# The first gate/up tile of each feed-forward as plain products, with one weight sum moved from an adding DMA to VectorE

## The chip, the cores and the metric

The kernel runs on one core of a Trainium2 chip. The metric is the device time of one execution in microseconds, as the median of several runs. The engines are named as in the profile: PE is TensorE (PEld its weight loads), DVE is VectorE, ACT is ScalarE, POOL is GpSimd, SP is SyncE, which here only issues DMAs.

## What is computed

A trunk of two layers over 512 tokens of width 1024, all in float32. Each layer is: half a feed-forward, a mixer, half a feed-forward.

```python
for layer in range(DEPTH):                      # DEPTH = 2
    x = x + FFN_RES * swiglu_ffn(rms_norm(x, ffn1_norm[layer]), ffn1_w_gate_up[layer], ffn1_w_down[layer])
    h = rms_norm(x, mix_norm[layer])
    y = swa_sink_attention(...) if kind == 0 else mla_attention(...)
    x = x + y
    x = x + FFN_RES * swiglu_ffn(rms_norm(x, ffn2_norm[layer]), ffn2_w_gate_up[layer], ffn2_w_down[layer])
return rms_norm(x, final_norm)

def swiglu_ffn(x, w_gate_up, w_down):           # 1024 -> 2 x 2816 -> 1024
    g, u = jnp.split(x @ w_gate_up, 2, axis=-1)
    return (jax.nn.silu(g) * u) @ w_down
```

So there are four feed-forwards, numbered f = 0 to 3 in the code, and two mixers between them.

## The kernel before

**Precision.** Every matmul operand is split in two parts: a high part that ACT writes by a copy (`high_fill`, `high_direct`, `high_mixed`) and a low part, the operand minus the high one, that DVE writes (`low_fill`, `low_direct`, `low_mixed`). A product is three matmuls: high by high, high by low, low by high (L1803 to L1805).

**Seven products in place of eight.** A feed-forward is cut into 30 units (`ffn_units`): 22 "G" units, each a tile of 128 gate and 128 up columns, and 8 "D" units of the down matrix, in the order G0-9, D, D, D, D, G10-17, D, D, D, D, G18-21. Within a unit the four weight blocks and the four quarters of the activations are combined by sums so that seven products (q = 1 to 7) of 128x256 columns replace eight: 7 x 4 chunks x 3 = 84 matmuls. The weight sums are made in SBUF. Four raw blocks per unit come from HBM: three lie in `plain` (loaded by SP in two DMAs, 512 and 256 KB), the fourth is loaded into `chain` and once more into `single`. POOL issues DMAs that add a further block to these (`accum_op`): three in turn to `chain` (`link`, steps 0, 1, 2; L754), one to `single` (`join`; L762). Each of the six weight operands of a unit is one fill: FA (two blocks, 128x1024) and FC from `plain`; FU, FB and FD from `chain` after its first, second and third sum; FE from `single`.

**Activations.** `h_mix` holds for each of four pairs of 128-column chunks three direct quarters and four sums of quarters (`mix`, three instructions on DVE, `x_sums`), each as high and low part. `pair_split` makes them in the order sums 0 and 1, direct low part, sum 2; then `high_mixed` (ACT) and `low_mixed` (DVE) split the sums.

**Order of the work.** It is written out by hand, and every engine runs its own list in order. On TensorE a unit is the products 1(u), 2(u), 4(u-1), 6(u), 3(u-1), 5(u), 7(u). In unit u DVE makes the low parts FU(u+1), FA(u+1), FC(u), FB(u+1), FD(u), FE(u+1), with the gate and up arithmetic in between; ACT writes the high parts in the same order, the copies s_1, u_2, u_3 of products 1, 6 and 7 (L957, L970, L991) that let the next product be added into the same bank, and the silu. Product 6 waits for s_1, product 7 for u_2, product 4 of the next unit for u_3. In eight units per feed-forward (3, 5, 7, 9, 14, 17, 19, 21, `COMBINED`) the hidden tiles of two G units are turned into direct quarters and sums for the D units, which adds `mix`, `high_direct`/`low_direct` and `high_mixed`/`low_mixed`.

**The beginning of a feed-forward.** `pairs_out` (ACT and DVE) evacuates the eight blocks that end the stage before: DVE adds a block to `xT` (L1297), ACT scales it with the gain (`gained`, L886) into `x_pair`, which has two buffers, and squares it for the norm; after each second block the pair is split. FA(0) and FU(0) are filled at the last block, ahead of its evacuation. TensorE runs the products 1, 2, 5 of unit 0 in `ffn`, then `sums` (the sum of squares, L1854), products 6 and 7, then `spread` (L1864), which brings the reciprocal root of the norm (POOL's `power`, then four small DVE instructions, `rms_values`) to all partitions, and goes on with unit 1. The first feed-forward has no stage before it: the tokens are loaded by DMA, transposed on TensorE (`x_transposed`, L1901) between the products of unit 0, and split in the same way.

**The down blocks and the rest of the weights** (`load`, `high`, `low`) pass through raw slots `w_raw`, which lie in `r_all`, the memory that also holds `plain`, `single` and the rotary tables; so their loads wait for the last fills of a feed-forward, and the first `plain` loads of the next one wait for the last splits of blocks. SP issues all these loads in order.

Of the kernel before, what the change touches and what calls it, by code (L numbers as in the profile page):

```python
# [13 lines left out]
P = 128  # L14
# [59 lines left out]
def fill_count(f, kind, u):  # L74

    at = {FU: 6 * u - 2 if u else 1, FA: 6 * u - 1 if u else 0, FB: 6 * u + 1 if u else 2, FE: 6 * u + 3,
          FC: 6 * u + 6 - 2 * (u == NU - 1), FD: 6 * u + 8 - 3 * (u == NU - 1)}[kind]
    return 6 * NU * f + at + 1


def product_order():
    out = [(q, 0) for q in (1, 2, 5, 6, 7)]
# [8 lines left out]
def product_count(f, q, u):  # L91

    return 7 * NU * f + PRODUCTS[q, u] + 1


def half_order():
    out = []
    for u in range(1, NU + 1):
        if u == 1:
            out.append((0, 0))  # L100
        if u < NU and UNITS[u][0] == "G":
            out.append((u, 0))
        if UNITS[u - 1][0] == "G":
            out.append((u - 1, 1))
# [6 lines left out]
def silu_order():  # L111
    out = []
    for u in range(1, NU):
        if u > 1 and UNITS[u - 2][0] == "G":
            out.append((u - 2, 1))
# [8 lines left out]
def half_count(f, u, half):  # L124

    return 2 * TILES * f + HALVES[u, half] + 1
# [5 lines left out]

def chain_count(f, u, steps):

    return 16 * (3 * ((NU * f + u) // CHAIN) + steps)


def single_count(f, u, steps):

    return 16 * ((NU * f + u) // SINGLE + steps)  # L140
# [144 lines left out]
def kv_interleaved(w, slot):  # L285

    return kv_raw(w, slot).rearrange("p (r t f) -> p r t f", t=2, f=HD)
# [21 lines left out]
def build(nc, x, gains, weights, a_sinks, consts, out):  # L309
# [3 lines left out]
    with ExitStack() as ctx:  # L313
# [52 lines left out]
        y_hi, y_lo = rows_of(y_all, 0, KD, S), rows_of(y_all, BIG, KD, S)  # L366
        h_mix, y_mix = (v[:, :].rearrange("p (k q l n) -> p k q l n", k=7, q=PAIRED, l=2) for v in (h_all, y_all))
# [4 lines left out]
        tables = r_flat[:, 8 * S:11 * S]  # L372
# [10 lines left out]
        x_pair = [view(4 * S + i * 2 * S, 4, HN) for i in range(2)]  # L383
        x_sum = view(8 * S, 4, HN)
        g_0 = [view(10 * S + i * HN, HN) for i in range(2)]
        g_1 = view(11 * S, HN)
        c_22 = [view(11 * S + (1 + i) * HN, HN) for i in range(2)]
        s_1, u_3 = view(11 * S + 3 * HN, HN), view(13 * S, HN)
# [45 lines left out]
        single_in = [sem(f"single_in{i}") for i in range(SINGLE)]  # L434
        chain_sum = [sem(f"chain_sum{i}") for i in range(CHAIN)]
        single_sum = [sem(f"single_sum{i}") for i in range(SINGLE)]
# [32 lines left out]
        gr_done = sem("gr_done")  # L469
        silu_done = sem("silu_done")  # L470
# [107 lines left out]
        def _(sp):  # L578
# [8 lines left out]
            def load_chain(f, u):  # L587

                g = NU * f + u
                if g >= CHAIN:  # L590
                    sp.wait_ge(fill_lo, fill_count((g - CHAIN) // NU, FD, (g - CHAIN) % NU))
# [6 lines left out]
            def load_single(f, u):  # L598

                g = NU * f + u  # L600
                if g >= SINGLE:
                    sp.wait_ge(fill_lo, fill_count((g - SINGLE) // NU, FE, (g - SINGLE) % NU))
                sp.dma_start(single[u % SINGLE], unit_source(f, u, A_21)).then_inc(single_in[u % SINGLE], 16)

            def load_plain(f, u):
# [3 lines left out]
                elif f > 0:  # L609
                    for i in ((3,), (0, 1), (1, 2))[u]:  # L610
                        sp.wait_ge(split_done, max(n for n in range(SEG_AT[f - 1], SEG_AT[f]) if slot(n) == i) + 1)
# [4 lines left out]
            def load_unit(f, u):  # L616

                if u == 0:
                    if f > 0:
                        sp.wait_ge(fill_lo, fill_count(f - 1, FC, NU - 3))  # L620
                    if f == 1:
                        sp.wait_ge(rot_done, 1 + PAIRS)
                        sp.wait_ge(t1_done, 1 + PAIRS)
                    if f == 3:
                        sp.wait_ge(mq_ready, 2)
                if f == 0 and u == 0:
                    load_plain(f, u)
                    load_x(2)
                    load_chain(f, u)
# [1559 lines left out]
```

## Time and profile before

| | us |
|---|---|
| three runs, median (lowest to highest) | 1867.21 (1865.55 to 1869.53) |
| profiled execution, its own time | 1863.95 |
| span of the profiled execution, first to last instruction | 1862.2 |
| PE busy | 1736.1 |
| DVE busy | 1424.5 |
| ACT busy | 962.8 |
| POOL busy | 447.9 |

The span lies in the profiled execution; the rest of its time is around it. PE busy counts a pipelined matmul from start to modelled end. The four feed-forwards take from the start to 362 us, 533 to 859, 904 to 1231 and 1486 to 1817 (without their down blocks); the mixers and the down blocks lie between them.

### The profile page before, as it was taken

What the parts mean: (1) busy time and instruction counts of PE and PEld (TensorE: products, weight loads), DVE (VectorE), ACT (ScalarE), POOL (GpSimd) and SP (SyncE); (2) the same over time, 40 slices, a digit from 0 to 9 for tenths busy, and PEclk for the clock granted to TensorE, in tenths of its full rate; (3) what the DMA queues carried; (4) which work ended last, traced back from release to release, by engine and by line L of the source; (5) the groups of instructions that cost most, each with busy time, mean ns of one, the idle gap of its engine ahead of it and who ended that gap; (6) DMA issues with size and microseconds to landing.
All of it is one profiled execution on the core that took longest, in us unless ns stands there. A gap on an engine that the chain in (4) does not pass through costs nothing. (4 is left out here: it accounts for less than half of the span.)

```text
span 1862.2 us, 34651 instructions
## 1 busy us (share of the span) xinstructions
PE 1736.1 (93%) x12889; PEld 1621.8 (87%) x12889; DVE 1424.5 (76%) x2796; ACT 962.8 (52%) x1904; POOL 447.9 (24%) x511
## 2 busy tenths in 40 slices
PE   5999999999969999999699999999999789999997
PEld 4999999977869999998599999987867689999995
DVE  5788787768668878866688778666896578878788
ACT  4554554446555545544455455444565455545452
POOL 1333333111023333330233333300000033333320
PEclk6999999999989999999899999999999899999999
DMA  6899999543359999993699999945112489999961
GB/s 177 204 214 235 230 221 231 151 113 86 108 128 231 221 227 229 223 204 107 163 231 218 223 221 229 212 117 130 29 42 66 117 190 219 224 224 224 231 157 69
DMA packets 189956, 329.42 MB, mean 177 GB/s; under 512 B 24865, under 2 KB 58846, under 8 KB 189790
## 3 DMA queue, kind: packets, MB, share of 16 engines
q0 software_dynamic: 69120, 125.86, 39.6%
q1 hardware_dynamic: 119104, 199.60, 33.9%
q8 instruction: 105, 1.72, 0.4%
q10 hardware_dynamic: 1566, 1.74, 0.3%
q14 instruction: 61, 0.50, 0.1%
HBM read 320.58 MB, written 2.10 MB: 173 GB/s over the span
## 5 line engine op out<-in xcount | busy, mean ns | idle before, releaser
L1803 PE MATMUL bank<-h_all,w_all 128*128 128x256 f32 x2464 | 711.6, 289 | 76.6 <-issue 28.7
L1804 PE MATMUL bank<-h_all,w_all 128*128 128x256 f32 x2464 | 704.9, 286 | 0.0
L1805 PE MATMUL bank<-h_all,w_all 128*128 128x256 f32 x2464 | 704.5, 286 | 0.0
L1803 PEld LDWEIGHTS bank<-h_all,w_all 128*128 128x128 f32 x2464 | 480.8, 195 | 88.3 <-issue 63.5
L1804 PEld LDWEIGHTS bank<-h_all,w_all 128*128 128x128 f32 x2464 | 481.0, 195 | 0.0
L1805 PEld LDWEIGHTS bank<-h_all,w_all 128*128 128x128 f32 x2464 | 480.8, 195 | 0.0
L754 POOL DMA_DIRECT2D work<-ffn_gu x264 | 231.7, 925 | 831.7 <-DVE w_all L1187 549.2
L868 ACT ACTIVATE w_all<-work 128x512 fp32r<-128x512 f32 x360 | 213.2, 622 | 322.1 <-DMA work<-ffn_gu 200.4
L1187 DVE TENSOR_TENSOR w_all<-work,w_all 128x512 fp32r<-128x512 f32 x360 | 243.9, 686 | 120.3 <-ACT w_all L868 120.1
L1187 DVE TENSOR_TENSOR w_all<-r_all,w_all 128x512 fp32r<-128x512 f32 (+1 forms) x360 | 310.7, 863 | 25.4 <-ACT w_all L868 20.1
L868 ACT ACTIVATE w_all<-r_all 128x512 fp32r<-128x512 f32 (+1 forms) x360 | 275.2, 767 | 84.9 <-PE bank L1805 84.1
L1803 PE MATMUL bank<-y_all,w_all 128*128 128x256 f32 x896 | 254.4, 284 | 11.4 <-DVE w_all L1187 11.4
L1804 PE MATMUL bank<-y_all,w_all 128*128 128x256 f32 x896 | 253.5, 283 | 0.0
L1805 PE MATMUL bank<-y_all,w_all 128*128 128x256 f32 x896 | 253.5, 283 | 0.0
L1803 PEld LDWEIGHTS bank<-y_all,w_all 128*128 128x128 f32 x896 | 171.9, 192 | 12.9 <-DVE w_all L1187 12.8
L1804 PEld LDWEIGHTS bank<-y_all,w_all 128*128 128x128 f32 x896 | 171.9, 192 | 0.0
L1805 PEld LDWEIGHTS bank<-y_all,w_all 128*128 128x128 f32 x896 | 171.9, 192 | 0.0
L945 ACT ACTIVATE work<-work 128x256 f32<-128x256 f32 x176 | 73.0, 417 | 143.7 <-DVE work L1354 143.4
L754 POOL DMA_DIRECT2D work<-ffn_d x96 | 87.3, 984 | 167.1 <-DVE w_all L1187 166.8
L1174 DVE TENSOR_TENSOR w_all<-r_all,w_all 128x1024 fp32r<-128x1024 f32 (+2 forms) x76 | 73.9, 972 | 57.2 <-ACT w_all L846 51.7
L762 POOL DMA_DIRECT2D r_all<-ffn_gu x88 | 86.3, 980 | 121.6 <-issue 120.8
L1341 DVE SCALAR_TENSOR_TENSOR xT<-bank,xT 128x256 f32<-128x256 f32 x224 | 93.7, 418 | 21.6 <-PE bank L1805 20.4
(186 smaller groups left out, 2591.3 us busy)
## 6 DMA issues: line engine op xcount, KB each, us to landing
work<-ffn_gu POOLq DMA_DIRECT2D x264, 256.0 KB, 5.8
r_all<-ffn_gu SPq DMA_DIRECT2D x88, 512.0 KB, 5.2
r_all<-ffn_gu SPq DMA_DIRECT2D x176, 256.0 KB, 5.9
work<-ffn_d POOLq DMA_DIRECT2D x96, 256.0 KB, 6.0
work<-ffn_gu SPq DMA_DIRECT2D x88, 256.0 KB, 5.6
r_all<-ffn_gu POOLq DMA_DIRECT2D x88, 256.0 KB, 6.9
r_all<-ffn_d SPq DMA_DIRECT2D x64, 256.0 KB, 5.6
r_all<-ffn_d SPq DMA_DIRECT2D x32, 512.0 KB, 5.2
```

The costliest lines, as they stand in the source:

```text
L754: pool.dma_start(chain[g % CHAIN], unit_source(f, u, slice(part * S, (part + 1) * S)), accum_op=ALU.add).then_inc(chain_sum[g % CHAIN], 16)
L762: pool.dma_start(single[u % SINGLE], unit_source(f, u, slice(0, S)), accum_op=ALU.add).then_inc(single_sum[u % SINGLE], 16)
L868: a.activation(hi, src, ACT.Copy).then_inc(fill_hi, 1)
L945: a.activation(buf, buf, ACT.Silu).then_inc(silu_done, 1)
L1174: last = v.tensor_tensor(w_lo[:, sl, 0:k, 0:m], w_raw[:, sl, 0:k, 0:m], w_hi[:, sl, 0:k, 0:m].bitcast(F32), ALU.subtract)
L1187: v.tensor_tensor(lo, src, hi.bitcast(F32), ALU.subtract).then_inc(fill_lo, 1)
L1341: return v.scalar_tensor_tensor(at, src, -0.5 if c < PAIRED else 0.5, at, ALU.mult, ALU.add)
L1803: t.matmul(o, wh, xh, start=c == 0 and not on, stop=False, skip_group_check=on)
L1804: t.matmul(o, wh, xl, start=False, stop=False, skip_group_check=on)
L1805: last = t.matmul(o, wl, xh, start=False, stop=c == PAIRED - 1, skip_group_check=on)
```

## The change

Unit 0 of each feed-forward (the first gate/up tile) is no longer made by the seven products. TensorE gets a new function that makes the gate tile and then the up tile, each 128x512, as plain products: 4 chunks x 2 blocks x 2 halves x 3 = 48 matmuls each. It needs only FA, FU and FC of unit 0, all of them raw blocks, and no sums of quarters; of the activations it needs the three direct quarters and the fourth quarter, which is split on its own into a new place, `early`, in `y_all`.

```diff
+            def plain_tile(f, up):
+                b = (C_BANKS if up else B_BANKS)[0]
+                pe.wait_ge(fill_lo, fill_count(f, FU if up else FA, 0))
+                if up:
+                    pe.wait_ge(fill_lo, fill_count(f, FC, 0))
+                places = ((1, 1), (2, 0)) if up else ((0, 0), (0, 1))
+                for c in range(PAIRED):
+                    if not up:
+                        pe.wait_ge(direct_lo, combine_count(f, c, False))
+                        pe.wait_ge(early_lo, PAIRED * f + c + 1)
...
             def ffn(f, m, ready):
-                if f > 0:
-                    pe.wait_ge(evac_done, ready - 2)
-                    for q in (1, 2, 5):
-                        product(f, q, 0, (0, PAIRED - 1))
-                    for q in (1, 2, 5):
-                        product(f, q, 0, (PAIRED - 1, PAIRED))
+                plain_tile(f, False)
                 sums(m, KD)
-                product(f, 6, 0)
-                product(f, 7, 0)
-                spread(m + 1)
+                plain_tile(f, True)
                 if f > 0:
                     pe.wait_ge(evac_done, ready)
-                for u in range(1, NU):
+                product(f, 1, 1)
+                spread(m + 1)
+                for q in (2, 6, 5, 7):
+                    product(f, q, 1)
+                for u in range(2, NU):
```

In `pairs_out` FA(0) moves one block ahead, FC(0) and the join of unit 1 are added, the sums of a pair (`pair_mix`) come after the direct and early parts of `pair_split`, and a mixed split comes after the evacuation of a block, not ahead of it. What is left of the last pair's sums and the fills of unit 1 move into `begin`, behind the end of `pairs_out`.

```diff
                 for j in range(KD):
                     if j >= begun:
                         low(n + j + AHEAD, end)
+                    if j == KD - 2:
+                        low_fill(f, FA, 0)
                     if j == KD - 1:
-                        low_fill(f, FA, 0)
                         low_fill(f, FU, 0)
-                    if j >= 3 and j % 2:
-                        q = (j - 3) // 2
-                        low_mixed(h_mix, combine_count(f, q, False), q)
+                        join(f, 1)
                     b = product(n + j)
                     v.scalar_tensor_tensor(xT[:, PERM[j], :], b[:, :], factor, xT[:, PERM[j], :],
                                            ALU.mult, ALU.add).then_inc(evac_done, 1)
+                    if j >= 3 and j % 2 and j < KD - 1:
+                        q = (j - 3) // 2
+                        low_mixed(h_mix, combine_count(f, q, False), q)
+                    if j >= 2 and j % 2 == 0:
+                        pair_split(f, j // 2 - 1)
+                        pair_mix(f, j // 2 - 1)
                     if j:
                         added(j == 1)
...
+            def begin(f, m):
+                def first():
+                    low_mixed(h_mix, combine_count(f, PAIRED - 1, False), PAIRED - 1)
+                    low_fill(f, FA, 1)
+                low_fill(f, FU, 1)
+                join(f, 2)
+                rms_values(m, D, first)
+                low_fill(f, FB, 1)
+                low_fill(f, FE, 1)
```

The gate of unit 0 is then normed over its whole width (`first_gate`), goes through silu on ACT and is multiplied with the up tile (`first_hidden`), all in unit 1. The first feed-forward has four pair buffers in place of two; its transposes run ahead of the tile, and its sums of pairs come behind all direct parts.

In the other units the sum of FE, an adding DMA of POOL onto a second load of the fourth block, becomes one DVE instruction: `chain` plus a block of `plain` into `single`. The second load goes too. As the first link changes `chain`, POOL's first link of a unit waits for this `join`; before, it waited only for the load of `chain`.

```diff
-            def load_single(f, u):
...
-                sp.dma_start(single[u % SINGLE], unit_source(f, u, A_21)).then_inc(single_in[u % SINGLE], 16)
...
                 if step == 0:
-                    pool.wait_ge(chain_in[g % CHAIN], 16 * (g // CHAIN + 1))
+                    pool.wait_ge(joined, order_of(f, u) + 1)
...
+            def join(f, u):
+                g = NU * f + u
+                dve.wait_ge(chain_in[g % CHAIN], 16 * (g // CHAIN + 1))
+                dve.wait_ge(plain_in[(u + 2) % 3], unit_count(f, u))
...
+                v.tensor_tensor(single[u % SINGLE], chain[g % CHAIN], plain[(u + 2) % 3][:, 0:S], ALU.add
+                                ).then_inc(joined, 1)
...
                     low_fill(f, FA, u + 1)
+                    join(f, u + 2)
```

The raw slots of the blocks move from `r_all` to `x_f`, except for the last segment. Their loads wait for the last product 7 of the D units, and the first `plain` loads of the next feed-forward wait for fills of this one instead of splits of blocks. The rotary tables (768 KB after the first feed-forward, 256 KB after the third) are loaded one unit later and ahead of the blocks.

```diff
-        w_raw = r_all[:, 0:SLOTS, :].rearrange("p s (k m) -> p s k m", m=P)
+        w_raw = x_f[:, :, :].rearrange("p a s -> p (a s)").rearrange("p (s k m) -> p s k m", s=SLOTS, m=P)
...
-                    sp.wait_ge(fill_lo, fill_count(f, FE, NU - 2))
+                    sp.wait_ge(fill_lo, fill_count(f, FE, NU - 1))
                     sp.dma_start(tables[:, part * S:3 * S], consts[:, P + part * S:]).then_inc(t_in, 16)
```

The remaining lines of the diff renumber counters and semaphores to the new order.

## Rows read from the trace of the kernel before

**Rows 1.** The page: span, and busy time with share and instructions of each engine
```profile
span 1862.2 us, 34651 instructions
...
PE 1736.1 (93%) x12889; PEld 1621.8 (87%) x12889; DVE 1424.5 (76%) x2796; ACT 962.8 (52%) x1904; POOL 447.9 (24%) x511
```

**Rows 2.** Waits of TensorE: line, releaser, us in total, times, longest
```profile
PE bank L1803 <- issue: 28.7, 5, 10.5
...
PE bank L1803 <- ACT work L991: 25.1, 27, 1.8
...
PE bank L1864 <- DVE st L1261: 12.5, 3, 4.6
```

**Rows 3.** Windows: busy us of PE, PEld, DVE, ACT, POOL; PEclk, DMA share
```profile
560.00:620.00 60.00, 59.99 (x501) 59.81 (x500) 50.39 (x98) 35.31 (x69) 20.87 (x24) 1.00 0.98 229
...
893.60:934.20 40.60, 23.68 (x157) 23.13 (x157) 27.62 (x48) 19.33 (x33) 10.78 (x12) 0.79 0.77 181
```

**Rows 4.** Timeline of TensorE: start, us, operation [idle before <- releaser]
```profile
47.04 1.84 PE L1854 MATMUL bank<-ones,acc 128*128 128x1 f32 x8 [5.66 <-DVE acc L1230]
...
65.86 0.28 PE L1803 MATMUL bank<-h_all,w_all 128*128 128x256 f32 x1
...
524.79 0.39 PE L1760 MATMUL bank<-y_all,w_all 128*128 128x512 f32 x1
...
562.74 0.28 PE L1803 MATMUL bank<-h_all,w_all 128*128 128x256 f32 x1
...
893.22 0.39 PE L1760 MATMUL bank<-y_all,w_all 128*128 128x512 f32 x1
...
904.08 0.55 PE L1803 MATMUL bank<-h_all,w_all 128*128 128x256 f32 x1 [10.47 <-issue]
...
921.57 1.12 PE L1864 MATMUL bank<-ident,st 128*128 128x128 f32 x4 [4.58 <-DVE st L1261]
...
934.21 0.28 PE L1803 MATMUL bank<-h_all,w_all 128*128 128x256 f32 x1
...
1476.68 0.39 PE L1760 MATMUL bank<-y_all,w_all 128*128 128x512 f32 x1
...
1515.54 0.28 PE L1803 MATMUL bank<-h_all,w_all 128*128 128x256 f32 x1
```

**Rows 5.** Timeline of ACT and DVE at the third beginning
```profile
900.72 1.06 ACT L875 ACTIVATE h_all<-work 128x1024 fp32r<-128x1024 f32 x1 [1.89 <-DVE work L1203]
...
902.75 1.22 DVE L1187 TENSOR_TENSOR w_all<-r_all,w_all 128x1024 fp32r<-128x1024 f32 x1 [2.07 <-ACT w_all L868]
...
905.63 0.68 DVE L1297 SCALAR_TENSOR_TENSOR xT<-bank,xT 128x512 f32<-128x512 f32 x1
```

**Rows 6.** DMA queues and issues of 960:1000, then 533:541
```profile
q0 software_dynamic: 2168, 3.94, 57.9%
...
q1 hardware_dynamic: 2106, 4.89, 37.8%
...
work<-ffn_gu POOLq DMA_DIRECT2D x12, 256.0 KB, 5.8
...
work<-ffn_gu POOLq DMA_DIRECT2D x1, 256.0 KB, 3.7
```

**Rows 7.** Timeline of DVE and ACT over two units
```profile
979.86 0.68 DVE L1187 TENSOR_TENSOR w_all<-work,w_all 128x512 fp32r<-128x512 f32 x1
...
980.47 0.42 DVE L1398 TENSOR_TENSOR work<-bank,work 128x256 f32<-128x256 f32 x1
...
985.45 1.16 ACT L868 ACTIVATE w_all<-work 128x512 fp32r<-128x512 f32 x2 [2.19 <-DMA work<-ffn_gu]
...
986.11 0.69 DVE L1187 TENSOR_TENSOR w_all<-work,w_all 128x512 fp32r<-128x512 f32 x1 [1.17 <-ACT w_all L868]
...
989.02 0.69 DVE L1187 TENSOR_TENSOR w_all<-work,w_all 128x512 fp32r<-128x512 f32 x1
...
1000.95 0.68 DVE L1187 TENSOR_TENSOR w_all<-work,w_all 128x512 fp32r<-128x512 f32 x1
```

More of the change, by code:

```diff
@@ L91, in product_count @@
 def product_count(f, q, u):
[L93 removed]
+    return len(PRODUCTS) * f + PRODUCTS[q, u] + 1
 def half_order():
@@ L112, in silu_order @@
     out = []
-    for u in range(1, NU):
-        if u > 1 and UNITS[u - 2][0] == "G":
+    for u in range(2, NU):
+        if u > 2 and UNITS[u - 2][0] == "G":
             out.append((u - 2, 1))
@@ L948, in ffn @@
                 end = SEG_AT[f + 1]
-                for u in range(NU):
-                    gate, before = UNITS[u][0] == "G", u > 0 and UNITS[u - 1][0] == "G"
-                    at = NU * f + u
+                begin(f)
+                for u in range(1, NU):
+                    gate, before = UNITS[u][0] == "G", u > 1 and UNITS[u - 1][0] == "G"
+                    at = order_of(f, u)
                     b = B_BANKS[u % 2]
@@ L961, in ffn @@
                     if u == 1:
-                        silu(f, 0, 0)
-                    if gate and u > 0:
+                        act.wait_ge(z_gate, f + 1)
+                        a.activation(z_0, z_0, ACT.Silu).then_inc(z_silu, 1)
+                    if gate:
                         silu(f, u, 0)
@@ L1790, in product @@
                     b = B_BANKS[u % 2]
-                fresh = u == 0 or (not gate and UNITS[u - 1][0] == "G")
+                fresh = u == 1 or (not gate and UNITS[u - 1][0] == "G")
                 for c in range(*part):
@@ L1807, in product @@
                     last.then_inc(prod_done, 1)
[L1809 to L1815 removed]
+            def plain_tile(f, up):
[8 more added lines that the diff above has]
+                        pe.wait_ge(early_lo, PAIRED * f + c + 1)
+                    for e, (i, j) in enumerate(places):
+                        wh, wl = (w_all[:, i, low, j * S + c * P:j * S + (c + 1) * P] for low in range(2))
+                        for half in range(2):
+                            o = b[:, half * HN:(half + 1) * HN]
+                            if half and not e:
+                                xh, xl = early[:, c, 0, :], early[:, c, 1, :]
+                            else:
+                                d = D_B11 if not e else (D_B22 if half else D_B21)
+                                xh, xl = h_mix[:, d, c, 0, :], h_mix[:, d, c, 1, :]
+                            first, end = c == 0 and not e and not half, c == PAIRED - 1 and e == 1
+                            t.matmul(o, wh, xh, start=first, stop=False, skip_group_check=half == 1)
+                            t.matmul(o, wh, xl, start=False, stop=False, skip_group_check=half == 1)
+                            last = t.matmul(o, wl, xh, start=False, stop=end, skip_group_check=half == 1)
+                        if c == PAIRED - 1 and (e or up):
+                            last.then_inc(prod_done, 1)
```

290 lines of the change are left out of this document (163 added, 127 removed).

## Prediction

> **What bounds the kernel now.** I read the page first: TensorE is busy for 1736 of 1862 us, so any gain has to come from its gaps or its work [rows 1]. The TensorE waits tell where the gaps are [rows 2]: 28.7 us in five waits of up to 10.5 us and 12.5 us in three waits for `st`, nearly all where a feed-forward begins, and 25.1 us in 27 small waits for ACT's copy u_3 (L991), spread over the units. Between those, a stretch of 60 us holds 501 matmuls [rows 3]: one takes 0.12 us, a unit of 84 takes 10.08 us, and nothing can be won there. In the same stretch the DMA engines are at 0.98: saturated, though TensorE does not wait for them directly.
>
> The third feed-forward shows a beginning [rows 4]: the last matmul of the block before starts at 893.22 (it ends at 893.6), unit 0 begins at 904.08 after 10.47 us idle, the spread of the norm waits another 4.58 us, and unit 2 begins at 934.21. That is 40.6 us for 144 matmuls worth 17.3. A matmul lasts 0.55 us at 904.08 and 0.28 us at 934.21: the granted clock over this stretch is 0.79 [rows 3], so part of it runs at the lower level, 1.2 GHz, after the idle time. From last matmul to unit 2 the second feed-forward takes 37.6 us (525.2 to 562.74), the fourth 38.5 (1477.1 to 1515.54); the first reaches unit 2 at 65.86 [rows 4].
>
> Why TensorE stands there is in DVE's and ACT's rows [rows 5]. The first weights (FA) get their low part at 902.75, because ACT split the third pair's sums first (900.72, 1.06 us, itself 1.89 us behind DVE's last sum). DVE evacuates the last block only at 905.63, twelve us after TensorE finished it.
>
> **The change, part by part.** *TensorE's work.* Unit 0 goes from 84 to 96 matmuls: 12 x 0.12 = 1.44 us in each feed-forward, 5.8 in all, all on the path; it is inside the sums below.
>
> *The beginnings.* The plain tile needs no sums of a pair, only the pair and one early quarter of it. I walk through the third one with durations of the rows (start to start: 0.60 us for 128x512 on DVE, 0.34 for 128x256, 0.87 for the direct part, 1.13 for 128x1024; ACT 0.5 to 1.0), in the new program order. FA is split one block sooner, at 897.8, so TensorE starts near 897.9, after some 4.8 us idle, and goes through pairs 0 to 2. The last evacuation comes at 904.0 (before: 905.63; FA, FU, the new join at 0.60 and two early splits are ahead of it, one mixed split is not). Then gain 0.7, ACT direct and early 1.2, DVE direct and early 1.3 with their handovers: pair 3 is ready at 907.5. TensorE's last quarter (12 matmuls at the lower level after the wait, an estimated 0.12 x 0.55 / 0.28 = 0.23 each: 2.8), the sums (0.9) and the up tile (1.4 for six slow matmuls, 5.0 for the rest) end near 917.6. The norm is computed under the up tile: DVE's values at 912.6, POOL's power by 914.5, four small steps by 915.7. So the 4.58 us wait for the spread should vanish. Products 1, spread and 2 of unit 1 end near 921.0, 6 and 5 near 924; product 7 waits about 1 us for ACT, which has the new full-width gate in front (norm, silu). Unit 2 begins near 926.3: 7.9 us earlier than 934.21. The second and fourth have the same chain behind their last evacuation, and a table load for silu in it (1.3 us); the same steps give 556.7 and 1509.7 against 562.74 and 1515.54: 6.0 and 5.8. In the first, the transposes no longer stand behind products and the sums of squares end at 42.5; before, TensorE's sums began at 47.04 after waiting 5.66 for them [rows 4]; unit 2 comes at about 61.0 instead of 65.86: 4.8. Sum: 24.5 us. Bounds: were there no waits at all, the third would need 20.2 us instead of 40.6, the other three about as much, and the gain would be near 75; were the pair order to cost DVE more than it frees, it could fall to some 8.
>
> *DMA removed.* Per unit one plain load of 256 KB and one adding DMA go. In a saturated window of 40 us the adding queue moved 3.94 MB (15 DMAs) in 57.9% of the engines' time, 1.54 us each; the plain queue 4.89 MB (18.7 pieces of 256 KB) in 37.8%, 0.81 each [rows 6]. Per unit 4 x 1.54 + 5 x 0.81 = 10.2 us of 10.08 becomes 3 x 1.54 + 4 x 0.81 = 7.9: from saturated to 78%. An adding DMA lands 5.8 us after its issue in the loaded window, 3.7 with nothing else in flight [rows 6]. I take 4.0 for the change, near the idle end, since the moved link finds little else in flight.
>
> *The join on DVE.* A 128x512 instruction with two SBUF operands lasts 0.69 us and 0.61 from start to start (979.86, 980.47) [rows 7]; 29 units x 4 = 116 of them, 70 us of DVE. DVE is the tight engine where units with pair sums (3, 5, 7, 9 and 14, 17, 19, 21) alternate with plain ones: from FU's low part to the next FU it takes 9.16 us (979.86 to 989.02) and then 11.93 (to 1000.95), 21.09 a pair against TensorE's 20.16 [rows 7]; the excess is what L991's waits show, 6 pairs x 4 with about 1 us. In the plain unit DVE idles 1.17 us before 986.11, because ACT waited for the adding DMA of FB until 985.45 [rows 7]. The join takes 0.60 in each unit: in the plain one it fits into that idle time if the DMA lands sooner, in the other it adds in full (12.53).
>
> *The moved link.* The first adding DMA of unit u+2 used to be issued behind the one before it on POOL's queue; now it waits for the join, 3.2 us after FU's low part, and ACT's FU of the next unit waits for its landing. Queued behind ACT's wait are s_1 (TensorE's product 6 waits for it) and FA; behind POOL's, the third link, which is not due. The loop is 3.2 + 0.35 wake-up + landing + 0.75 on ACT + 0.6 on DVE: 4.9 + landing. At 4.0 it is 8.9, a pair is 8.9 + 12.5 = 21.4, 1.25 over TensorE; x 24 pairs = 30 us, 5 more than now. Against that, the irregular waits for late DMAs behind the 25.1 (units outside this pattern, most of them in the fourth feed-forward) should go: about 8. Steady units: -3, say 0, with 24 us for each us of landing: 3.7 gives -10, 4.7 +14, 5.8 +40.
>
> The Trainium skill says (DMA: Bandwidth & Descriptors, "Latency and other measured facts") that a DMA's fixed cost shrinks when HBM is lightly loaded; the two landings of [rows 6] agree in direction. Its fit for a DMA issued from GpSimd ("Anatomy of one DMA") would give an estimated 2.6 us for 256 KB, under the 3.7 of the row; with it the loop would be 7.5 us and never bind.
>
> *Raw blocks in other memory.* The down blocks' loads start earlier; nothing waits for them now. The rotary tables after the first and third are loaded a unit later and ahead of the first block: in the first (768 KB) ACT waits for that block in unit 29, and u_2 and product 7 behind it; 1 to 3 us, I take 2, in the third none. Early splits on ACT and DVE (0.34 each, 16 of them) are in the walk above. The SP queue loses a load and the waits before it: free.
>
> Sum against the profiled execution, 1863.95 us by its time (span 1862.2): 1863.95 - 24.5 + 0 + 2 = 1841.5. The median of the runs is 3.3 above the profiled one, so 1845 for a median.
>
> **Rivals.** *The link behind the join binds (slower).* Place: ACT's FU of every plain unit. It decides from the landing at which steady units lose the 22 us that the beginnings win: (25 + 8 + 22) / 24 = 2.3 us a pair, a loop near 9.95, a landing of 5.0 without the 8 us, 4.7 if late DMAs stay. At the loaded 5.8 the pair is 23.2: 73 us of waits instead of 25, 1890. For it: the landing is 5.8 today, the plain loads start 1.5 us after the join. Against: a fifth of the DMA time is gone. Chance 0.14.
>
> *The relief wins in the steady units too.* Landing falls to 3.7: the loop is 8.6, DVE alone binds (8.4 + 12.53 = 20.93), 0.8 to 0.95 a pair, and the irregular waits go: -10, to 1835, with better beginnings (a DVE that is less far behind) 1825. Chance 0.22.
>
> *The wait is only moved at the beginnings.* The DVE and ACT chain that evacuates the blocks stays; if pair 3 comes at the old 909, or the clock stays low through the up tile (42 matmuls more at 0.23 instead of 0.12: 4.6 us), each beginning gains 2 to 3: 10 us in all, 1860 to 1865. Chance 0.14.
>
> **How the numbers follow.** The forecast, 1845, has 0.50; its own range is 1836 to 1856. Range for 8 in 10: 1827 to 1872, from the good end of the relief to the link at a landing of 4.9. A difference of about 0.2% (3.7 us) is what a measurement of this kernel can tell from none. Faster: 0.50 + 0.22 + half of the moved wait, less a little for the forecast's own tail, 0.76; same 0.10; slower 0.14.
>
> **What the profile after would show.** TensorE's wait before the first tile at 5 us or less, no wait for `st`, unit 2 some 8 us sooner in the third; DMA share near 0.8 in the steady stretches, adding DMAs landing at about 4; waits for L991 of about 1 to 1.5 us after units 5, 7, 9, 17, 19, 21. Waits of TensorE for s_1 (L957 before) and of ACT for `work` at FU would mean that the link binds; first waits still of 8 us and a low clock through the up tile, that the beginnings did not move.

## The result and the profile after

The change made the kernel slightly slower: 1873.36 us against 1868.64 us, medians of 20 runs each, taken beside one another, ratio 1.0027 with a 95% interval of 1.0016 to 1.0038. I had forecast 1845, faster. By the bound that I gave (0.2%) this is slower, and it lies above my range.

The page of the changed kernel: span, busy times, the two DMA queues (packets, MB, share of 16 engines' span) and two landings:

```profile
span 1872.5 us, 34649 instructions
...
PE 1750.5 (93%) x12937; PEld 1634.8 (87%) x12937; DVE 1484.5 (79%) x2892; ACT 958.6 (51%) x1892; POOL 331.1 (18%) x379
...
q0 software_dynamic: 50112, 91.25, 29.1%
q1 hardware_dynamic: 101824, 168.13, 28.9%
...
work<-ffn_gu POOLq DMA_DIRECT2D x252, 256.0 KB, 4.6
...
work<-ffn_d POOLq DMA_DIRECT2D x96, 256.0 KB, 5.0
```

TensorE's longest waits in it (line, releaser, us in total, times, longest), to be read beside [rows 2]:

```profile
PE bank L1881 <- ACT work L1011: 33.0, 29, 2.0
PE bank L1881 <- DVE w_all L1207: 16.5, 12, 1.4
PE bank L1908 <- DVE y_all L1252: 14.7, 5, 5.4
PE bank L1956 <- DVE acc L1274: 14.7, 1, 14.7
PE bank L1908 <- DVE w_all L1207: 10.2, 3, 4.8
```

The waits for `st` and the waits of 10.5 us are gone, as intended; the 14.7 us at L1956 lie in the first feed-forward, where TensorE comes to the sums of squares sooner and waits for them longer (5.66 us before, [rows 4]). The wait for u_3 (L1011, before L991) rose from 25.1 to 33.0 us.

Where the time went can be read from the starts of the matmuls: a unit is 84 of them, so every 84th start of L1881 to L1883 is the start of a unit. I use five sums over the four feed-forwards: "beginnings" is the time from the last block's end (in the first: from zero) to unit 2; the others are what units take over 10.08 us each. "D units" stands for 10 to 13 and 22 to 28: eight D units and the G units that follow the second group; "29" is unit 29. In us, from one profiled execution of every kernel of this study:

| kernel | ratio to before [95%] | beginnings | units 2–9 | 14–21 | D units | 29 |
|---|---|---|---|---|---|---|
| before | 1 | 182.5 | 12.8 | 9.0 | 23.6 | 4.5 |
| the change | 1.0027 [1.0016, 1.0038] | 166.6 | 24.6 | 7.4 | 34.4 | 8.5 |
| plain_tile_alone | 0.9916 [0.9894, 0.9937] | 161.0 | 16.8 | 12.6 | 23.7 | 9.5 |
| join_alone | 1.0014 [0.9994, 1.0034] | 173.8 | 15.8 | 8.3 | 37.5 | 4.5 |
| join_own_copy | 0.9933 [0.9910, 0.9956] | 165.5 | 19.9 | 6.6 | 27.5 | 8.3 |
| join_on_pool | 1.0150 [1.0124, 1.0176] | 162.1 | 33.8 | 19.3 | 38.9 | 9.8 |
| plain_tile_tables | 0.9886 [0.9856, 0.9916] | 159.7 | 15.5 | 13.2 | 25.1 | 4.5 |
| hybrid_tables | 0.9827 [0.9803, 0.9851] | 161.5 | 14.9 | 4.0 | 23.8 | 4.5 |
| join_sooner | 0.9933 [0.9912, 0.9954] | 163.2 | 17.3 | 6.6 | 31.5 | 9.7 |
| spare_add | 0.9960 [0.9944, 0.9976] | 155.7 | 23.6 | 12.4 | 28.0 | 9.7 |
| after_filled | 0.9983 [0.9968, 0.9998] | 159.6 | 26.8 | 11.9 | 31.6 | 7.0 |
| hybrid_filled | 0.9811 [0.9793, 0.9830] | 152.7 | 16.8 | 3.3 | 26.1 | 4.5 |

Between the two profiled executions the span grew by 10.3 us: beginnings −15.9, units +25.2, the rest +1.0. By the medians the difference is 4.7 us; the profiled execution of before lies 4.7 us under its median of these runs, that of the changed kernel 1.0 above its own, so about half of the 10.3 is scatter between executions. Single cells scatter too: after_filled, which differs from the change at the beginnings alone, has 2.2 us more in units 2–9, 4.4 more in 14–21 and 2.9 less in the D units. I rest on ratios, and on cells only where several kernels say the same.

### The profile page after: what moved, and what is told of

It is laid out like the page before. It is cut to its first block and busy times, and to the rows that moved or that the text cites. A ratio compares the mean times of both kernels' runs of the same rounds, so it can differ in the third digit from the quotient of the medians.

```text
span 1872.5 us, 34649 instructions
## 1 busy us (share of the span) xinstructions
PE 1750.5 (93%) x12937; PEld 1634.8 (87%) x12937; DVE 1484.5 (79%) x2892; ACT 958.6 (51%) x1892; POOL 331.1 (18%) x379
## 5 line engine op out<-in xcount | busy, mean ns | idle before, releaser
L1881 PE MATMUL bank<-h_all,w_all 128*128 128x256 f32 x2352 | 670.7, 285 | 42.3 <-ACT work L1011 33.0
L1882 PE MATMUL bank<-h_all,w_all 128*128 128x256 f32 x2352 | 666.7, 283 | 0.0
L1883 PE MATMUL bank<-h_all,w_all 128*128 128x256 f32 x2352 | 666.6, 283 | 0.0
L1881 PEld LDWEIGHTS bank<-h_all,w_all 128*128 128x128 f32 x2352 | 452.4, 192 | 50.0 <-issue 34.1
L1882 PEld LDWEIGHTS bank<-h_all,w_all 128*128 128x128 f32 x2352 | 452.8, 193 | 0.0
L1883 PEld LDWEIGHTS bank<-h_all,w_all 128*128 128x128 f32 x2352 | 452.6, 192 | 0.0
L766 POOL DMA_DIRECT2D work<-ffn_gu x252 | 219.8, 872 | 1014.6 <-DVE w_all L1207 513.9
L870 ACT ACTIVATE w_all<-work 128x512 fp32r<-128x512 f32 x352 | 209.3, 624 | 334.9 <-DMA work<-ffn_gu 203.3
L1207 DVE TENSOR_TENSOR w_all<-work,w_all 128x512 fp32r<-128x512 f32 x352 | 238.8, 687 | 100.9 <-ACT w_all L870 100.0
L1881 PE MATMUL bank<-y_all,w_all 128*128 128x256 f32 x896 | 256.2, 286 | 18.5 <-DVE w_all L1207 11.4
L1883 PE MATMUL bank<-y_all,w_all 128*128 128x256 f32 x896 | 253.3, 283 | 0.0
L1881 PEld LDWEIGHTS bank<-y_all,w_all 128*128 128x128 f32 x896 | 171.6, 191 | 24.4 <-DVE w_all L1207 16.9
L1883 PEld LDWEIGHTS bank<-y_all,w_all 128*128 128x128 f32 x896 | 171.7, 192 | 0.0
L1194 DVE TENSOR_TENSOR w_all<-x_f,w_all 128x1024 fp32r<-128x1024 f32 (+2 forms) x72 | 69.1, 959 | 61.0 <-ACT w_all L845 55.5
L1834 PE MATMUL bank<-y_all,w_all 128*128 128x512 f32 x272 | 107.3, 395 | 1.3 <-DVE w_all L1194 1.3
L1836 PE MATMUL bank<-y_all,w_all 128*128 128x512 f32 x272 | 106.0, 390 | 0.0
```

What stands on the lines that cost most here:

```text
L766: pool.dma_start(chain[g % CHAIN], unit_source(f, u, slice(part * S, (part + 1) * S)), accum_op=ALU.add).then_inc(chain_sum[g % CHAIN], 16)
L870: a.activation(hi, src, ACT.Copy).then_inc(fill_hi, 1)
L1194: last = v.tensor_tensor(w_lo[:, sl, 0:k, 0:m], w_raw[:, sl, 0:k, 0:m], w_hi[:, sl, 0:k, 0:m].bitcast(F32), ALU.subtract)
L1207: v.tensor_tensor(lo, src, hi.bitcast(F32), ALU.subtract).then_inc(fill_lo, 1)
L1834: t.matmul(b[:, :], wh, hi[:, c, :], start=c == 0, stop=False)
L1836: last = t.matmul(b[:, :], wl, hi[:, c, :], start=False, stop=c == k - 1)
```

## The experiments

Theories: (A) the join's time on DVE makes the units longer; (B) the units pay for the beginnings, because DVE and ACT enter unit 2 with work left over; (C) the first link, moved behind the join, comes too late.

### The plain tile without the join

```diff
-                    pool.wait_ge(joined, order_of(f, u) + 1)
+                    pool.wait_ge(chain_in[g % CHAIN], 16 * (g // CHAIN + 1))
...
+                pool.dma_start(single[u % SINGLE], unit_source(f, u, slice(0, S)), accum_op=ALU.add
+                               ).then_inc(single_sum[u % SINGLE], 16)
...
-                    join(f, u + 2)
```

> The changed kernel with FE's sum back where it was: a second load of the fourth block and an adding DMA of POOL; the first link waits only for its load again, DVE has no join. Between the two profiles the stretches from a feed-forward's start to its unit 2 got 15.9 us shorter in all, and the units from 2 to 29 got 25.3 us longer. Theory A (the join on DVE makes the units longer): the beginnings keep their 16 us, units 2 to 29 come back to the 1191 us of the kernel before, ratio 0.991 to 0.993. Theory B (the units pay for the beginnings: DVE and ACT enter unit 2 with work left over, whatever makes the join): units 2 to 9 stay some 10 us longer, ratio 0.997 to 1.000. The DMA share of a steady stretch goes back to 0.95 or more under both.

Measured: 0.9916, 1853.8 us. The beginnings are 21.5 us shorter than before. The D units are back at 23.7; units 2–9 keep 4.0 of their 11.8 us, and unit 29 is still 5.0 over before. So the plain tile, with the raw blocks in their new place, is good for some 16 us, and the other half of the change loses more than that. Mostly A or C, with a little of B.

### The join without the plain tile

```diff
+                dve.wait_ge(plain_in[(u + 2) % 3], unit_count(f, u))
...
+                v.tensor_tensor(single[u % SINGLE], chain[g % CHAIN], plain[(u + 2) % 3][:, 0:S], ALU.add
+                                ).then_inc(joined, 1)
...
+                    if u >= 2:
+                        pool.wait_ge(joined, joined_count(f, u))
```

> The kernel before with only the join of units 2 to 29 on DVE and the link behind it; beginnings, raw blocks and tables as they were. Theory A (join, or the link behind it): units 2 to 29 get 15 to 25 us longer, ratio 1.008 to 1.013. Theory B (the units pay for the beginnings): units 2 to 9 keep their 13 us of excess, only the D units and the last ones lose, 5 to 10 us, ratio 1.003 to 1.005. If the relief of the DMA engines is worth what my second rival said, ratio 0.995 or less.

Measured: 1.0014, and the interval takes in 1: less than A's or B's number, more than the relief's, so a miss for all three. The D units lose 14 us (the change: 10.9); units 2–9 lose 3.0, where the change loses 11.8. The beginnings gain 8.7 us in this profile, though nothing of them was moved: the wait for `st` is 7.9 us instead of 12.5; the reason is open. So in units 2–9 the parts don't simply add: the join costs little after the old beginnings and much after the new ones.

### The same join, with the link let go

```diff
-                    pool.wait_ge(joined, order_of(f, u) + 1)
+                    pool.wait_ge(chain_in[g % CHAIN], 16 * (g // CHAIN + 1))
...
-                v.tensor_tensor(single[u % SINGLE], chain[g % CHAIN], plain[(u + 2) % 3][:, 0:S], ALU.add
+                v.tensor_tensor(single[u % SINGLE], single[u % SINGLE], plain[(u + 2) % 3][:, 0:S], ALU.add
```

> The changed kernel, with the fourth block loaded a second time into the place of the sum, so that the join adds in place and the first link waits for its load alone, as in the kernel before. It takes one plain load of 256 KB per unit more (DMA share 0.77 to some 0.85). If the link behind the join costs (theory C), the units lose little or none of their 25 us, ratio 0.990 to 0.994; if the join's time on DVE costs (theory A) or the beginnings' leftover work (B), the ratio stays at 1.002 to 1.004.

Measured: 0.9933. With the join on DVE as in the change, and one load more, the kernel is 0.94% faster than the change: some 17.6 us. The released link is the one difference that lets work start sooner, so the price is the link's. C.

The loop itself can be read in a D unit of the changed kernel (third feed-forward). Timeline of DVE, ACT and POOL (start, us, operation, idle before and its releaser):

```profile
1037.26 0.68 DVE L1207 TENSOR_TENSOR w_all<-work,w_all 128x512 fp32r<-128x512 f32 x1
...
1040.76 0.69 DVE L1225 TENSOR_TENSOR r_all<-work,r_all 128x512 f32<-128x512 f32 x1
...
1048.18 0.69 DVE L1207 TENSOR_TENSOR w_all<-work,w_all 128x512 fp32r<-128x512 f32 x1 [0.76 <-ACT w_all L870]
...
1047.51 0.63 ACT L870 ACTIVATE w_all<-work 128x512 fp32r<-128x512 f32 x1 [1.16 <-DMA work<-ffn_d]
...
1041.85 0.86 POOL L766 DMA_DIRECT2D work<-ffn_d  x1 [2.68 <-DVE r_all L1225]
```

FU's low part at 1037.26, the join at 1040.76, the link at 1041.85; it lands 5.6 us later, when ACT, which has waited for it, starts FU of the next unit at 1047.51; DVE, which waits for ACT, follows at 1048.18. That is 10.9 us from FU to FU, where TensorE has 10.08. Over all 32 D units it is 10.36 us on average, but this average (and the landing of 5.45 us in it) mixes two kinds. In the first D unit of each group (10 and 22) the link lands in 3.7 us and nothing waits for it: 9.3 us. In the other 24 it is 10.71 us: 2.9 to the join, 0.7 of join, 0.4 to the link, a landing of 6.03 (5.64 to 6.55), and 0.7 for ACT and the handover; ACT idles 1.76 us and DVE 1.35 us ahead of FU. In the plain units of the pairs (6, 8, 18, 20) the landing is 3.9 on average and DVE idles 0.3 us. Over units 3 to 29, ACT's idle time ahead of FU is 64 us in the change, 11 before and 0 in join_own_copy; DVE's, ahead of FU's low part, is 48 us in the change, 6 before; ahead of FB's it fell from 109 to 37: the stall changed its place.

### The join sooner

```diff
                     low_fill(f, FU, u + 1)
+                    if u > 2 and u not in COMBINED:
+                        join(f, u + 2)
...
-                    join(f, u + 2)
+                    if u <= 2 or u in COMBINED:
+                        join(f, u + 2)
```

> The changed kernel with the join directly behind FU's low part in the units without pair sums, instead of behind FA's, some 2.4 us sooner; FA and the join wait for the first plain load alone, FC for the second. In the changed kernel the D units last 10.33 and 10.39 us from FU to FU, with 1.0 us of DVE idle ahead of FU: the loop over the moved link is 3.0 (FU to join) + 0.6 + 0.4 + 5.45 (landing) + 0.8. If that loop is the cost (theory C), it falls to about 8 us, the idle time goes and the kernel comes to 1857 to 1862, ratio 0.993 to 0.996, near join_own_copy. If DVE's time for the join is the cost (theory A), 1.001 to 1.004 as it is.

Measured: 0.9933, as C says. The same D unit, DVE and ACT:

```profile
1035.43 0.68 DVE L1208 TENSOR_TENSOR w_all<-work,w_all 128x512 fp32r<-128x512 f32 x1
1036.03 0.69 DVE L1226 TENSOR_TENSOR r_all<-work,r_all 128x512 f32<-128x512 f32 x1
...
1045.52 0.68 DVE L1208 TENSOR_TENSOR w_all<-work,w_all 128x512 fp32r<-128x512 f32 x1
...
1044.45 0.61 ACT L871 ACTIVATE w_all<-work 128x512 fp32r<-128x512 f32 x1
```

No engine waits at FU any more; the period is 10.09 us. (So that the join can come so early, FA and the join wait here for the first of the two plain loads alone, in every unit; this is not separated from the earlier join.) DVE's idle time ahead of FU in units 3 to 29 falls from 48 to 3 us. Units 2–9 gain 7.3 us, the D units 3.0 (with the link free altogether 4.7 and 7.0). Unit by unit the loop's share is plainer: units 11 to 13 and 23 to 25, the D units behind the first of each group, are over 10.08 us by 5.4 us in all in the change, 7.7 in join_alone and 4.5 in after_filled, by 0.2 or less before, in join_own_copy, in join_sooner and in spare_add, and by at most 1.4 in any other kernel. Two different ways of making the link earlier gave the same 0.9933: C holds, and its place is the loop over FU.

### The price of the join's time

```diff
                     low_fill(f, FA, u + 1)
+                    if u > 1:
+                        v.tensor_tensor(acc[:, :], r_x[:, :], r_x[:, :], ALU.add)
```

> plain_tile_alone with one more DVE instruction in each unit from 2 on, at the join's place: it adds two 128x512 operands in SBUF and its result is not used. No DMA goes and no link moves, so it shows the price of the join's time on DVE alone. Where DVE is the tight engine (32 units with pair sums), it should add its 0.60 us in full, and in the 16 D units at the edge some more: 12 to 22 us, ratio 0.998 to 1.003. If DVE has room in both units of a pair, 0.992 to 0.994.

Measured: 0.9960, between the two expectations. Against plain_tile_alone one more instruction in each of 112 units (67 us of DVE) costs 7.4 us by the medians, 8.2 by the ratios: 6.8 us more in units 2–9, 4.3 in the D units, nothing in 14–21. The D units' 4.3 lie in units 10 and 22, where the excess is 25.8 us instead of 21.4; the change has 26.9 there. A holds for a part; in most units DVE had room.

These runs make a ladder, here by the ratios: plain tile and raw blocks −15.7 us (0.9916), the join's time +8.2 (0.9960), fewer DMAs −5.0 (0.9933, join_own_copy; its interval overlaps the one before), the link behind the join +17.6 (1.0027).

### The join on POOL

```diff
-                v.tensor_tensor(single[u % SINGLE], chain[g % CHAIN], plain[(u + 2) % 3][:, 0:S], ALU.add
+                g.tensor_tensor(single[u % SINGLE], chain[g_ % CHAIN], plain[(u + 2) % 3][:, 0:S], ALU.add
```

> The changed kernel with the join as an instruction of POOL (128x512; such an instruction lasts 1.38 us there, 1.0 us more than it has waited for on DVE in its own time of 0.6). DVE loses 70 us of work; the link comes later by some 0.8 us less what the join waited in DVE's order. Theory A: units 2 to 29 come back to 1191 us or below, ratio 0.988 to 0.993. Theory C: the link is no earlier, 1.002 to 1.006. Theory B: 0.997 to 1.000. If an instruction of POOL slows DVE's beside it, DVE's 128x512 instructions get longer than 0.69 us.

Measured: 1.0150, above all the numbers expected, but on the side of the last sentence. DVE has 2776 instructions, as many as in plain_tile_alone, but is busy for 1554.2 us instead of 1417.5. Groups of DVE instructions (busy, mean ns of one), of plain_tile_alone:

```profile
L1240 DVE TENSOR_TENSOR w_all<-r_all,w_all 128x1024 fp32r<-128x1024 f32 x120 | 146.4, 1220 | 15.3 <-ACT w_all L903 15.2
L1411 DVE SCALAR_TENSOR_TENSOR xT<-bank,xT 128x256 f32<-128x256 f32 x224 | 94.0, 419 | 21.2 <-PE bank L1893 20.2
...
L1465 DVE TENSOR_TENSOR work<-work 128x256 f32<-128x256 f32 x84 | 35.7, 425 | 2.9
```

and of join_on_pool:

```profile
L1228 DVE TENSOR_TENSOR w_all<-r_all,w_all 128x1024 fp32r<-128x1024 f32 x120 | 187.1, 1559 | 18.8 <-ACT w_all L891 18.8
...
L1453 DVE TENSOR_TENSOR work<-work 128x256 f32<-128x256 f32 x84 | 92.8, 1105 | 2.9
L1399 DVE SCALAR_TENSOR_TENSOR xT<-bank,xT 128x256 f32<-128x256 f32 x224 | 91.5, 417 | 22.8 <-PE bank L1881 22.8
```

Instructions with two operands in SBUF got longer where a join runs beside them: of the 84 in the last row of plain_tile_alone, the 41 that overlap a join in join_on_pool last 1818 ns on average, the 43 others 425 as before. FU, FB and FD (128x512), which hardly ever run beside a join, kept their 0.69 us (687 and 685 ns). Those with one operand in PSUM did not get longer (417 and 419 ns), beside a join or not. The Trainium skill (SBUF — State Buffer, "Who interferes with whom") says that a DVE instruction with two SBUF inputs contends with a GpSimd instruction that reads SBUF, and calls the ports that they share an exclusive lock; the rows agree.

### The tables behind the first blocks

```diff
-                if part is not None:
                 for j in range(KD):
+                    if part is not None and j == SLOTS:
```

> plain_tile_alone (0.9916 of the kernel before) with the rotary tables' load moved behind the loads of the first four down blocks. In plain_tile_alone unit 29 is over its 10.08 us by 4.01 us in the first feed-forward and 2.51 in the third, 0.72 in the second, where no table is loaded. If the tables ahead of the first block are the cause, both fall to about 0.7 and the kernel gains 4 to 5 us: 1849, ratio 0.989. If unit 29 waits for something else, the ratio stays at 0.9916.

Measured: 0.9886, and unit 29 takes 0.73 us over 10.08 in the first and third feed-forward instead of 4.01 and 2.51. In ACT's waits for the raw down blocks (`x_f`), plain_tile_alone has this row, and plain_tile_tables no such row:

```profile
ACT w_all L878 <- DMA x_f<-ffn_e: 11.8, 2, 6.6
```

The unit's excess shows the tables' price; the ratios alone would not, as their intervals overlap.

### The join by turns

```diff
+                if u not in BY_DVE:
+                    return
+                dve.wait_ge(single_in[u % SINGLE], single_count(f, u))
...
-                if u >= NU:
+                if u >= NU or u in BY_DVE:
```

> The same, but the joins that fall into units without pair sums (the D units and every second G unit) are DVE instructions in place on the second load; the 44 others (those in units with pair sums and at the beginnings) stay adding DMAs of POOL. No link waits for a join. DVE has idle time in just those units (1.17 us ahead of FB's low part before), so the join should cost nothing there, and the DMA engines lose 72 adding DMAs of 1.54 us. If the late DMAs of the saturated stretches are what is left to gain, 2 to 5 us less than plain_tile_tables, ratio 0.986 to 0.988; if DVE's time is what counts in every unit, 3 to 6 us more, 0.991 to 0.993.

Measured: 0.9827, better than expected, and faster than both kernels. Units 14–21 fall from 13.2 to 4.0 us over their 10.08, and DVE's idle time ahead of FB's low part there from 34 to 16. The DMA share of a steady stretch (windows: busy us of PE, PEld, DVE, ACT, POOL; PEclk, DMA share) of plain_tile_alone:

```profile
560.00:620.00 60.00, 58.61 (x486) 58.46 (x487) 50.83 (x97) 35.65 (x71) 20.16 (x23) 1.00 0.95 221
```

and of hybrid_tables:

```profile
560.00:620.00 60.00, 59.38 (x494) 59.06 (x492) 52.60 (x100) 33.86 (x67) 16.63 (x20) 1.00 0.92 210
```

The links issued in 14–21 land sooner, in 5.59 us on average instead of 5.95. So taking adding DMAs away is worth something, where it is bought with DVE time that was idle and with no wait in the chain. Whether the gain comes from the DMA engines or from POOL's queue, which issues one DMA less in these units, was not taken apart.

### TensorE kept busy at the beginnings

```diff
+                for _ in range(count):
+                    t.matmul(MISC[:, 0:P], ones[:, :], ones[:, :], start=True, stop=True)
```

> The changed kernel with TensorE kept busy where it waits at the beginnings: products of a matrix of ones into an unused bank, 14 of some 0.31 us each ahead of the last pair's quarter of the gate tile (second to fourth feed-forward), and 14 and 9 ahead of the first weights of the third and fourth. In the changed kernel a matmul of 128x256 lasts 0.21 us instead of 0.12 from that quarter on, at a granted clock of 0.62 in the third beginning (913.4 to 926). If that lower level comes from the waits (4.8, then 2.81 us there) and is the step at which the third beginning missed, the stretch from the last quarter to unit 1 falls from 12.6 to about 10 us in the third, likewise in the others: 6 to 10 us in all, ratio 0.997 to 1.000. If the chain of DVE and ACT sets the end of this stretch anyway, 1.002 to 1.004 as it is.

Measured: 0.9983, as expected. Windows of TensorE over the third beginning (busy us, matmuls; PEclk, DMA share), in the changed kernel: the wait for FA, pairs 0 to 2 with the wait for pair 3, from the last quarter to unit 1, unit 1:

```profile
898.60:903.40 4.80, 0.00 (x0) 0.91 0.00 0
903.40:913.40 10.00, 7.19 (x37) 0.67 0.16 28
913.40:926.00 12.60, 12.60 (x70) 0.62 0.59 134
926.00:934.70 8.70, 7.82 (x64) 1.00 0.30 49
```

and about the same stretches of after_filled:

```profile
899.40:904.20 4.80, 3.15 (x30) 1.00 0.00 0
904.20:912.50 8.30, 7.68 (x64) 1.00 0.02 2
912.50:922.30 9.80, 8.13 (x68) 1.00 0.66 160
922.30:931.70 9.40, 8.24 (x67) 1.00 0.51 84
```

With the waits filled the clock stays at the upper level, 2.4 GHz, and the third beginning takes 32.3 us instead of 36.1. In the second and fourth a wait of 2.27 us is left ahead of pair 3; 10 and some 22 matmuls behind it still take 0.21 us, and these beginnings take 31.0 and 33.8 us instead of 33.5 and 34.9.

> hybrid_tables (ratio 0.9827) with the same fillers. There the lower level lasts some 9 us behind the waits of 4.8 us in the second and fourth beginning and 3 us behind the 2.39 us in the third; at 0.12 instead of 0.21 us a matmul that is some 4, 4 and 1.3 us: 1829, ratio 0.977 to 0.980. If the fillers only delay TensorE, 0.983 to 0.985.

Measured: 0.9811, above the range expected, against 0.9827 without the fillers: the direction is right, but the intervals overlap, so a gain is not shown. The beginnings are 8.8 us shorter in the profile, but the units take 3.3 us more, 1.9 of it in 2–9. In both kernels with fillers units 2–9 grew when the beginnings shrank (by 2.2 and 1.9 us); that fits B, but is no more than cells scatter.

## Why the prediction was wrong, step by step

Three steps failed. The moved link was checked in the pairs alone, with a landing of 4.0 us, so the units outside them were to gain (the D units lost 10.9 us). Units 2 to 9 had no term for the lead that DVE loses by a shorter beginning (they lost 11.8 us). And the beginnings left out most of the slow matmuls behind a wait (15.9 us won instead of 24.5).

**The beginnings: mechanism right, 24.5 us was 15.9.** By feed-forward 3.8, 4.1, 4.5 and 3.6 us instead of 4.8, 6.0, 7.9 and 5.8. TensorE and DVE in the third, to be read beside [rows 4, 5]:

```profile
903.41 0.58 PE L1908 MATMUL bank<-h_all,w_all 128*128 128x256 f32 x1 [4.81 <-DVE w_all L1207]
...
913.39 0.55 PE L1908 MATMUL bank<-h_all,w_all 128*128 128x256 f32 x1 [2.81 <-DVE y_all L1252]
...
909.53 0.68 DVE L1340 SCALAR_TENSOR_TENSOR xT<-bank,xT 128x512 f32<-128x512 f32 x1
...
912.83 0.42 DVE L1252 TENSOR_TENSOR y_all<-work,y_all 128x256 fp32r<-128x256 f32 x1
```

Up to here the walk held: 4.81 us of idle time (4.8 predicted, though from 893.6 to my 897.9 it is 4.3), pair 3 ready 14.7 us after the last block's end (13.9 by the walk), no wait for `st`, and later a unit 1 of 8.9 us (8.7). The step that failed is the next one: "six slow matmuls, 5.0 for the rest" of the up tile. After its wait of 2.81 us TensorE stayed at the lower level, 1.2 GHz, through the last quarter and half of the up tile's 48 matmuls, where I had six: 12.6 us at a granted clock of 0.62, where I had 10.1. In the second and fourth beginning the waits are 5.40 and 2.88 us, and the matmuls behind them take 0.21 us as well. I had this as a part of the third rival, at 4.6 us a beginning, and after_filled shows that it was the clock: its beginnings are 7.0 us shorter in all, of the 8.6 that were missing.

**The DMA load: right.** I said 0.78; steady stretches show 0.73 and 0.76:

```profile
560.00:620.00 60.00, 55.98 (x461) 55.29 (x460) 51.94 (x97) 34.39 (x69) 14.78 (x17) 1.00 0.73 162
1020.00:1060.00 40.00, 37.40 (x306) 36.67 (x305) 32.85 (x65) 17.35 (x27) 9.72 (x12) 1.00 0.76 179
```

**The pairs: nearly right.** From FU to FU on DVE, units 3, 5, 7, 17 and 19 and the plain units behind them take 12.99 + 8.83 = 21.82 us on average; I had 21.4. Before, the same ten units give 21.44 a pair, where I had read 21.09 from one pair; so a pair grew by 0.38 us, and I had 0.31. The adding DMAs land in 4.0 us there, the value that I took; issues of the changed kernel in 960:1000, as in [rows 6]:

```profile
work<-ffn_gu POOLq DMA_DIRECT2D x11, 256.0 KB, 4.0
```

**The units outside the pairs: the largest miss.** I credited 8 us there, for late DMAs that should go, and priced the link's loop only in the plain units of the pairs, 24 times over. In the D units behind the first of each group the link lands in 6.03 us, not 4.0, and the loop is 10.71 against TensorE's 10.08 (my formula, 4.9 + landing, gives 10.9; the join comes 0.3 us sooner behind FU there). The D units, with those behind them, lost 10.9 us instead of gaining 8: the instruction's time cost 4.3 by spare_add, in units 10 and 22, and letting the link go gave back 7.0 in join_own_copy, in the others. That is the slower rival's mechanism, in another place: I priced it for all pairs at one landing (1890) and didn't ask, unit by unit, at which landing a unit of 10.08 us stands still: 5.2. The signs that I had named for it came: TensorE's waits for s_1 rose from 1.1 us to 2.6, and ACT waits for `work` at FU.

That the landing is longer there goes with SP's plain loads. Two links of POOL and the first plain load behind each, in units 10 and 11 of the third feed-forward of the changed kernel:

```profile
1032.38 0.86 POOL L766 DMA_DIRECT2D work<-ffn_d  x1 [2.36 <-DVE r_all L1225]
...
1033.47 0.33 SPq L629 DMA_DIRECT2D r_all<-ffn_d  x1
...
1041.85 0.86 POOL L766 DMA_DIRECT2D work<-ffn_d  x1 [2.68 <-DVE r_all L1225]
...
1042.41 0.33 SPq L629 DMA_DIRECT2D r_all<-ffn_gu  x1
```

The first lands in 3.7 us, with the load 1.09 us behind it; the second in 5.6, with the load 0.56 us behind it. Of the 112 first links of units 2 to 29, 28 have the load 0.56 us behind and land in 5.64 to 7.80 us; the 84 others, with 1.09 us or more (or no load near), in 3.75 in the median, three of them above 5. The 28 are the links of units 13 to 15 and 25 to 28, issued two units before, mostly in D units. In join_on_pool the load comes 1.3 us or more behind 24 of these same 28, and they land in 3.76 us in the median, 4.77 at most. No run moved the loads alone, and other DMAs can delay a link too: in join_sooner 72 links with no plain load within 2.5 us behind them land in 5.06 in the median.

The relief itself is worth something where no wait pays for it: 14–21 gained 9.2 from plain_tile_tables to hybrid_tables. The 1.6 us that they gained in the change are within the scatter of these cells.

**Units 2 to 9: not in the sum at all.** I let a pair grow from 21.09 to 21.4 us wherever it stands, which is some 5 us for their 16 pairs; they lost 11.8. Before, unit 4, which follows the first unit with sums, was on time in three feed-forwards of four: DVE entered the units with a lead. In the change unit 4 is late by 1.1 to 1.5 us in the first three. In its fourth, unit 3 is late by 3.6 us instead. DVE's lead shows in FU's low part of unit 4, which ended 6.9 us before the unit began (7.1 in join_alone) and ends 6.1 before it in the change, and 5.6 to 6.6 in every kernel with the new beginnings. In join_alone, with the old beginnings, unit 4 loses only 0.2 in three of four. The runs divide the loss roughly: 4.0 us with the plain tile alone, 6.8 more with an idle DVE instruction at the join's place, and 4.7 less once the link is free; that is 3.7 us too many, which is what join_own_copy, with fewer DMAs, takes less there than spare_add.

**The rotary tables: half right.** Unit 29 is 2.1 us longer in the first feed-forward, as I said, and also in the third, where I said none: the tables' load waits for FE of unit 29, and the blocks' loads stand behind that wait in SP's queue, whatever the size of the tables. Their size counts for something in other kernels (4.01 and 2.51 us over 10.08 in plain_tile_alone).

By terms: beginnings −15.9 for −24.5, units 2 to 28 +21.2 for 0, unit 29 with the tables +4.0 for 2. The landing, from which I had the slower rival decided, was right where I looked; my 14% for that rival came from checking it against the pairs alone.

## What to carry to other kernels

When a step gets a new wait, work out its loop (from an instruction over the wait, the DMA and back to the same instruction one turn later) for each kind of turn, the light ones too: a light turn has the work to spare but not the latency. A stage that begins sooner hands its engines over with less lead, so the first turns behind it have to be priced with that, not with the steady excess. Before an operation is moved for good, move it only in the turns where the engine that takes it idles: 72 of the 116 joins on DVE gave 0.6% on top of the plain tile's gain; all 116 gave 0.17% of it back even with the link free (0.9933 against 0.9916, intervals overlapping), and with the link behind them turned it into a loss of 0.3%.

## What the hardware showed that I had not expected

The 116 joins as instructions of POOL cost DVE more than they save it: it is busy for 137 us more than in plain_tile_alone, and for 70 more than in the change, where it makes the joins itself (1554.2 against 1484.5); they last 1683 ns each on POOL. A wait of 2.4 us on TensorE was followed by 3 us of matmuls at the lower clock in the third beginning of plain_tile_alone, one of 2.8 us by some 9 us in the changed kernel; the wait's length alone does not decide it, as a wait of 2.27 us in after_filled was followed by 10 slow matmuls in the second beginning and by some 22 in the fourth. And an adding DMA of 256 KB did not land sooner than 3.52 us after its issue, in 348 of them; of the 116 first links of the change the median is 3.79, the ninetieth percentile 6.15; the Trainium skill's fit (DMA: Bandwidth & Descriptors, "Anatomy of one DMA") gives an estimated 2.6 us, which the trace does not bear out.
